# Hymba-style decoder step: sample attention by sample, its values gathered between later samples' keys

## The reference, cut to what matters

```python
D_MODEL, SEQ, DEC_BATCH, PAST_LEN, PAGE_SIZE = 1024, 512, 8, 4096, 128
N_HEADS, HEAD_DIM = 8, 64                  # cache: 320 pages of 128 x 8 x 64

def _fox_sample(q, k_new, v_new, logf_new, cache_k, cache_v, cache_logf, page_table):
    k_past = cache_k[page_table].reshape(bsz, past, N_HEADS, HEAD_DIM)
    v_past = cache_v[page_table].reshape(bsz, past, N_HEADS, HEAD_DIM)
    f_past = cache_logf[page_table].reshape(bsz, past, N_HEADS)
    ...
    cum = jnp.cumsum(jnp.concatenate([f_past, logf_new], axis=1), axis=1)
    s = jnp.einsum('bqhd,bkhd->bhqk', q, k_all) * (HEAD_DIM ** -0.5)
    s = s + cq - ck                        # forget sums behind each key
    p = jax.nn.softmax(s, axis=-1)
    return jnp.einsum('bhqk,bkhd->bqhd', p, v_all)

def _layer(x, c, ...):
    sh1, sc1, ga1, sh2, sc2, ga2 = _adaln(c, w_ada, b_ada, 6)
    h = _rms_norm(x, g_norm1) * (1.0 + sc1) + sh1
    q, k, v, logf, conv_in, gate_b = _mixer_inputs(h, w_in, b_forget)
    attn = attend(q, k, v, logf)           # prompt: causal, with the same forget sums
    conv_y, new_buf = _short_conv(conv_in, conv_buf, conv_w)
    x = x + ga1 * _merge_heads(attn, conv_y, gate_b, g_attn_out, g_conv_out, w_out)
    h = _rms_norm(x, g_norm2) * (1.0 + sc2) + sh2
    x = x + ga2 * _hier_moe(h, ...)        # top 2 of 32 experts, three 1 MB weights each
```

## Time and profile before

| | us |
|---|---|
| three runs | 1048.71, 1046.69, 1042.32 |
| their median | 1046.69 |
| span of the profiled execution | 1045.5 |
| TensorE busy | 847.3 (81%) |
| VectorE busy | 542.3 (52%) |
| POOL busy | 292.1 (28%) |
| ScalarE busy | 202.7 (19%) |
| moved by DMA | 318.40 MB, mean 305 GB/s |

### The profile page before, as it was taken

The page is one execution under the profiler, slowest core; times in us unless marked ns, Lnnn a source line. Parts: engine busy times, 40 slices in busy tenths (PEclk is TensorE's granted clock), DMA queues, the critical chain, the costliest instruction groups (busy, mean ns, idle before and its releaser), DMA issues.

```text
span 1045.5 us, 10030 instructions
## 1 busy us (share of the span) xinstructions
PE 847.3 (81%) x3810; PEld 371.9 (36%) x3810; DVE 542.3 (52%) x726; ACT 202.7 (19%) x385; POOL 292.1 (28%) x261
## 2 busy tenths in 40 slices
PE   7689999999457899998987989765888888778810
PEld 1144443444222334443232333223444444444300
DVE  1379999999999999642042020542111111111258
ACT  1321112100342322242000000121211222111111
POOL 4417632562101213102233232301222222221013
PEclk9689999999666575566999798876999999999955
DMA  9928778886779996616986999968999999999242
GB/s 332 399 90 290 285 281 340 275 304 207 261 276 335 371 382 249 222 41 256 361 341 267 359 333 358 373 254 294 389 410 413 412 411 412 412 412 413 107 176 82
DMA packets 79514, 318.40 MB, mean 305 GB/s; under 512 B 11090, under 2 KB 11110, under 8 KB 58473
## 3 DMA queue, kind: packets, MB, share of 16 engines
q1 hardware_dynamic: 52592, 163.56, 40.7%
q0 software_dynamic: 24576, 150.03, 38.3%
q10 hardware_dynamic: 2308, 4.31, 1.1%
HBM read 307.17 MB, written 14.85 MB: 308 GB/s over the span
## 4 chain that ended last, share of the span: by engine, by line
PE 65%; DMA 13%; DVE 11%; issue 6%; ACT 4%; SPq 1%; POOL 0%; ACTq 0%; POOLq 0%; DVEq 0%
PE bank L406 15%; PE bank L740 9%; PE bank L609 5%; PE bank L764 5%; DMA R_kv<-in_cache_v_dram,kv_index 5%; DMA R_w<-in_w_expert_up_dram 5%; PE bank L560 5%; PE bank L305 3%; PE bank L480 3%; PE bank L477 3%; PE bank L498 2%; DVE R_x L1232 2%; ACT R_h L861 2%; DMA R_w<-in_w_ada_dram 2%; DVE R_cm L1238 2%
## 5 line engine op out<-in xcount | busy, mean ns | idle before, releaser
L1732 POOL DMA_INDIRECT R_kv<-in_cache_k_dram,kv_index x64 | 98.6, 1540 | 244.6 <-DVE R_cm L1238 221.3
L1232 DVE TENSOR_TENSOR R_x<-R_kv,R_x 128x1024 f32<-128x1024 f32 x128 | 161.5, 1302 | 3.8 <-DMA R_x<-q_rows_scratch 3.8
L1238 DVE TENSOR_REDUCE R_cm<-R_x 128x16 f32<-128x1024 f32 x128 | 149.5, 1208 | 0.0
L406 PE MATMUL bank<-R_h,R_w 128*128 128x512 f32 x320 | 140.2, 599 | 1.2 <-ACT R_h L861 1.2
L1732 POOL DMA_INDIRECT R_kv<-in_cache_v_dram,kv_index x64 | 63.1, 986 | 166.3 <-PE bank L560 146.4
L560 PE MATMUL bank<-R_kv,R_cm 128*8 128x512 f32 x512 | 75.9, 676 | 19.8 <-DMA R_kv<-in_cache_v_dram,kv_index 19.6
L1808 POOL DMA_INDIRECT expert_rows_scratch<-R_h,R_part x32 | 32.0, 1001 | 211.6 <-DVE R_h L1593 204.2
L406 PEld LDWEIGHTS bank<-R_h,R_w 128*128 128x128 f32 x320 | 61.0, 192 | 79.9 <-issue 78.3
L1590 DVE COPY R_h<-bank 128x128 f32<-128x128 f32 x32 | 9.3, 292 | 147.0 <-PE bank L756 147.0
L305 PE MATMUL bank<-R_w,R_q 128*32 128x512 f32 x256 | 51.8, 938 | 13.8 <-DMA R_w<-in_w_ada_dram 8.2
L1593 DVE TENSOR_SCALAR R_h<-bank,R_part 128x512 f32<-128x512 f32 x32 | 24.0, 751 | 70.6 <-PE bank L764 70.6
(11 more groups left out here) (329 smaller groups left out, 1345.0 us busy)
## 6 DMA issues: line engine op xcount, KB each, us to landing
R_w<-in_w_ada_dram SPq DMA_DIRECT2D x24, 1024.0 KB, 8.1
R_w<-in_w_in_dram SPq DMA_DIRECT2D x12, 1024.0 KB, 7.7
R_w<-in_w_ada_final_dram SPq DMA_DIRECT2D x8, 1024.0 KB, 10.2
R_kv<-in_w_expert_gate_dram SPq DMA_DIRECT2D x8, 1024.0 KB
R_kv<-in_w_expert_up_dram SPq DMA_DIRECT2D x8, 1024.0 KB
R_kv<-in_w_expert_down_dram SPq DMA_DIRECT2D x8, 1024.0 KB
R_q<-in_w_expert_gate_dram SPq DMA_DIRECT2D x8, 1024.0 KB
R_q<-in_w_expert_up_dram SPq DMA_DIRECT2D x8, 1024.0 KB
```

The source lines that it names most:

```text
L406: last = nc.tensor.matmul(bank[m][:, :], l, r, start=(k == 0), stop=(k == KD - 1))
L1232: V.tensor_tensor(prod[:, r, :], kv_ring[:, n % RING, r, :], spread(q, [P, CH // 2, HW]), ALU.mult)\
L1238: V.reduce_sum(scores[:, b, lo:lo + CH // 2, :], prod[:, r, :].rearrange("p r (h d) -> p r h d", h=H), AX.X).then_inc(S["k_used"], 1)
L1732: pool.indirect_dma_start(kv_flat[:, g % RING, :], None, k_rows if g < NKV else v_rows, bass.IndirectOffsetOnAxis(kv_index[:, n:n + 1], 0))\
```

## The change

Keys and values share the four places in one order that is written out ahead (`kv_seq`): 16 key chunks, then values between keys, one value to 1.08 keys up to value 22, then one to one, and the last 18 values. Each sample has its own softmax, two key chunks after its last key: maximum (`sample_top`), reduction over partitions on POOL, subtraction (`sample_shift`), exponentials (`sample_exp`), sum (`sample_sum`). Value chunks stand on TensorE at 23 places inside sections 2 to 5, at each of the 32 attention steps, and nine behind them. Key products are written over the keys; the first sample's q is spread by a matmul. The log-forget sums and the new row are made on VectorE. Five modulation chunks move from attention into sections 0 to 2, with places of their own (`a_unit`). Sections use two PSUM banks in pairs, scores two and turned probabilities one. Output tiles stand whole behind each other, the samples ahead of tile 3, and routing is done once for all five tiles.

```diff
-        NEW_AT, DIAG_AT = 16, 32
-        ADA_AT = {w: n for n, w in enumerate((0, 1, 3, 4, 6, 8, 10, 12, 14, 16, 19, 22))}
+        def value_at(m):
+            if m < 5:
+                return 15.5 + m
+            if m < 23:
+                return 21.5 + (m - 5) * 19.5 / 18
+            return 41.0 + (m - 23)
+
+        order = sorted([(float(n), 0, n) for n in range(NKV)] + [(value_at(m) + 0.3, 1, m) for m in range(NKV)])
+        kv_seq = [(("k", "v")[kind], i) for _, kind, i in order]
+        ring_slot = [g % RING for g in range(2 * NKV)]
+        ring_prev = [g - RING if g >= RING else None for g in range(2 * NKV)]
...
+        EARLY = 5
+        ADA_AT = {w: EARLY + n for n, w in enumerate((7, 10, 12, 15, 17, 20, 22))}
+        VALUES_AFTER = {2: (3, 4, 5, 6, 7), 3: (1, 2, 3, 5, 6, 7), 4: (1, 2, 3, 5, 6, 7), 5: (1, 2, 3, 5, 6, 7)}
+        LATE = (0, 1, 2, NT, 3)
...
             def prompt_section(s):
+                for pair in range(2):
+                    for half in range(2):
+                        w = use_unit(8 + 2 * s + half)
+                        for m in (2 * pair, 2 * pair + 1):
+                            e = 4 * s + m - 2
+                            if half == 0 and 0 <= e < 16:
+                                pe.wait_ge(S["acc_act"], e + 1)
+                            if half == 0 and e >= 16:
+                                pe.wait_ge(S["acc_dve"], e - 15)
...
+                            block = 4 * pair + 2 * half + m % 2
+                            if block in VALUES_AFTER.get(s, ()):
+                                values(1)
+                    if pair == 0 and s < 3:
+                        early_ada(2 * s)
+                if s < 2:
+                    early_ada(2 * s + 1)
...
             for w in range(NT * H):
                 turn(w)
                 if w + 2 < NT * H:
                     score(w + 2)
-                if w >= NT * H - V_EARLY:
-                    value_chunk(w - (NT * H - V_EARLY))
+                values(1)
                 weigh(w)
...
+            values(1)
+            turn_output(NT - 1)
+            values(1)
+            spread_chunk(2)
...
+            gather_values(6)
+            for half in range(2):
+                for k0 in range(0, KD, 2):
+                    out_part(0, half, k0)
+                    if next_v[0] < NKV:
+                        values(1)
+            sample_sums()
+            gather_values(7)
+            for t in (1, 2):
+                for half in range(2):
+                    for k0 in range(0, KD, 2):
+                        out_part(t, half, k0)
+                turn_rows(t - 1)
+                route(t - 1)
+                if t == 1:
+                    sample_head_squares()
+            out_samples()
+            for half in range(2):
+                for k0 in range(0, KD, 2):
+                    out_part(3, half, k0)
+            for i in (2, 3, 4):
+                turn_rows(i)
+                route(i)
...
             def k_chunk(n):
...
-                for i in range(2):
-                    if n:
-                        dve.wait_ge(S["k_used"], 2 * n - 1 + i)
-                    r = slice(i * CH // 2, (i + 1) * CH // 2)
-                    V.tensor_tensor(prod[:, r, :], kv_ring[:, n % RING, r, :], spread(q, [P, CH // 2, HW]), ALU.mult)\
-                        .then_inc(S["k_products"], 1)
+                keys = kv_ring[ring_slot[g]]
+                V.tensor_tensor(keys[:, :, :], keys[:, :, :], spread(q, [P, CH, HW]), ALU.mult).then_inc(S["k_products"], 1)
+                dve.wait_ge(S["k_products"], n + 1)
+                V.reduce_sum(scores[:, b, s * CH:(s + 1) * CH, :], keys.rearrange("p r (h d) -> p r h d", h=H), AX.X)\
+                    .then_inc(S["k_used"], 1)
...
+            def decay_step(i):
+                d = 1 << i
+                out = decay[:, :, 0:PPP - d, :]
+                last = V.tensor_tensor(out, out, decay[:, :, d:PPP, :], ALU.add)
...
             def cache_chunk(g):
-                n = g % NKV
-                if g >= RING:
-                    pool.wait_ge(*((S["k_used"], 2 * (g - RING + 1)) if g - RING < NKV else (S["v_used"], g - RING - NKV + 1)))
+                kind, n = kv_seq[g]
+                if ring_prev[g] is not None:
+                    before, i = kv_seq[ring_prev[g]]
+                    pool.wait_ge(S["k_used" if before == "k" else "v_used"], i + 1)
...
+            for g in range(RING, 2 * NKV):
+                kind, n = kv_seq[g]
+                if kind == "k" and n % NCH == 0:
+                    query(n // NCH)
                 cache_chunk(g)
+                for b in turn_after.get(g, ()):
+                    pool.wait_ge(S["top_part"], b + 1)
+                    G.partition_all_reduce(top_all[:, b, :], top[:, b, :], P, RED.max).then_inc(S["top_ready"], 1)
...
-            free = ((S["v_used"], NKV), (S["wo_part_done"], 2), (S["lg_done"], 5), (S["h2_ready"], 5))
+            free = ((S["v_used"], NKV), (S["wo_done"], 2 * NT), (S["lg_done"], 5), (S["h2_ready"], 5))
```

830 lines of the change are left out of this document (472 added, 358 removed).

## The result

The changed kernel takes 1091.6 us (median of four runs, 1086.3 to 1096.5), the kernel before, run beside it, 1047.2 (four runs, 1042.3 to 1048.7): a ratio of 1.043, 95% interval 1.038 to 1.048. It is slower by 44 us, where 12 us less were forecast, and lies above the forecast's range. The profiled execution spans 1084.1 us; the one before spanned 1045.5. In all that follows medians count every run, while ratios and their intervals leave out the slow runs, those over 1.5% above the fastest run of the same kernel.

The account below looks back on a forecast made before the run. No single engine was full throughout; VectorE was the clock before the loop, weights paced the experts. +47 until the loop, +29 in it and -87 behind gave -11: 1034.5 us profiled, 1035 as median, range 1005 to 1064.

Parts of the forecast that it names:

- The rest, 0: Experts and last norm, after the tables are copied out: no change from 330.3 us.
- Behind the loop, 141: From the loop's last weighing to the tables: 227.7 us falls to 141, with only 9 value chunks left there.
- The term of 6 us for each of two turns: Behind the loop: turn and route of a tile between output tiles, waiting for a norm, 6 us each, 12 together.
- Until the loop, 47 more: From the start to the first row maximum: 274.65 us grows to 322.
- At 175: Before the loop: VectorE at its 18th key chunk at 167 us, 175 with waits for forget path and ring.
- All of them at 6.4: From 175 us to the loop: 23 pairs of key and value at 6.4 us each.
- (landing + 4.53)/2: Ring before the loop: least cost of a key and value pair; a landing of 8.3 us gives 6.4.
- The loop, 29 more: The 32 attention steps: 212.9 us grows to 242, as 63 + 118 + 61.
- In place, the same cost: Key products before the loop: writing over the key chunk costs the same 4.53 us, a gain of at most 0.1.
- Log-forget sums, +5 net: Before the loop: additions moved to VectorE add 9.2 + 2.2 us; POOL's removed additions give back about 6.
- B: Rival, sections and loop: the ring costs more than it gives, pairs above 6.7 us, 1074 us; chance 0.18.
- A: Rival, loop: mostly full TensorE clock, loop 219 us, total 1012 us; chance 0.22.

Follow-up runs that it names:

- e11_act: On e4_three, ScalarE's copy of a tile's turned rows put ahead of the next tile's norm, first two tiles behind the loop; 1043.7 us, ratio to kernel before 0.997.
- e1_order: Changed kernel with early modulation chunks 1 and 3 moved behind the forget gate's projection and the turns of the log-forget rows; 1074.7 us.
- e4_three: Changed kernel with all three edits (e1_order, e2_ring5, e3_conv) in one kernel; 1048.0 us, ratio to kernel before 1.001.
- e6_early0: Changed kernel with no modulation chunks beside the sections, all twelve back in the loop; 1074.3 us, ratio to kernel before 1.033.
- e2_ring5: Changed kernel with a fifth place in the key and value ring, given up after the last key; 1074.5 us, ratio to kernel before 1.033.
- e3_conv: Changed kernel with the value chunk of loop steps 0 to 4 moved behind the sums of the convolution's squares; 1074.7 us, ratio to kernel before 1.030.
- b1_inplace: Kernel before with only the key product written over the key chunk, one whole product and reduction instead of two halves; 1051.4 us, ratio 1.008.
- e7_poolsum: Changed kernel with the five doubling additions over the log-forget sums back on POOL; 1091.3 us, ratio to kernel before 1.044.
- e5_late: On e4_three, eight of the sixteen value chunks of loop steps 8 to 23 moved behind the loop; 1046.9 us, ratio to kernel before 1.004.

## Why the prediction was wrong, step by step

**The rest, 0: nearly right** (+3.6 us in the one execution; 331.4 with three edits, so part of it is spread between executions; where the remainder lies wasn't looked for). No term of the sum stood for it.

**Behind the loop, 141: right in sum** (142.3, and 141.9 to 148.3 over ten traces with the clock; the bounds were 135 and 152). The term of 6 us for each of two turns was seen as such: 3.6 of it is the wait, of which e11_act removed 2.4.

**Until the loop, 47 more: the step that failed** (81.6 more). Three terms of it, with 20.4 + 8.5 + 5.3 us:
- "At 175": the working, 62 + 18 x 4.53 + 23, has 18 chunks done by then, so it answers to the start of the 19th, and with 23 more the count of 41 before the loop is right. The 19th starts at 195.4, +20.4. With the order mended it starts at 176.4 (e1_order), with all three edits at 173.2 (e4_three): the count of the work was right, and what failed was that the early modulation chunks were taken to delay nobody. The prediction said of the early modulation units that "each is due a whole section before its successor is needed". That was an argument on SP's queue alone. It left out that a unit's buffer is free only with the chunk before, that on the chain the landing is 12 to 14 us (the page's median is 11.6 for these units, 9.2 for one in R_w), and that the forget gate's projection and the log-forget rows stand behind these chunks on TensorE, with VectorE waiting for both (e1_order, e6_early0).
- All of them at 6.4: one is 14.9, where VectorE does the convolution's products between two key chunks, +8.5. In the kernel before the same gap is there, 14.8 us (238.01 to 252.85), so the old trace had this term. With four places just two keys are ahead, so little is stored up in this time.
- The pair itself: 6.64 for the other 22, +5.3 (356.3 - 195.4 - 14.9 = 146.0, over 22). To 240 us, where bytes bind, it is the forecast's 6.4; most of the excess is the 10 pairs behind, at 6.8, where the transfers had room and a fifth place helped. The landing on the chain is 9.3 us rather than 8.3, and POOL's issue, 0.94 to 2.9 us, was priced in the text but is not in (landing + 4.53)/2. With both in, that formula gives 7.4 and more, so it isn't confirmed either: not every pair waits for a landing on the chain. In the last pairs VectorE waits 4.1 us for a section's matmuls, which stand behind a value chunk that has not landed. With five places a pair is 6.2 (e2_ring5) and 6.4 (e4_three), counted the same way.

**The loop, 29 more: failed in its first eight steps** (38.8 more). Steps 24 to 31 were right, and so were steps 8 to 23 (114.4 for 118, bound by bytes as forecast). Steps 0 to 7 got 3 us more for the softmax pieces and took 15.8. The term left out is the value chunk in the chain of the convolution's norm: 6.9 of it (e3_conv). The other 6 weren't told apart; with that edit what remains over the kernel before lies mostly in steps 0 and 1 (3.1 and 2.1 us).

**In place, the same cost: right for VectorE's rows, wrong for POOL's** (b1_inplace). **Log-forget sums, +5 net:** about right at the 18th key chunk (6.0 earlier without them), though the time shows nothing of it (e7_poolsum).

**The rivals.** B came nearest: slower, and with pairs of 7.0 us on average against its limit of 6.7, though its 1074 is 18 us short. That it is so near is in part luck: its mechanism is the 14 us that a fifth place gives back, of some 41. The delay at 175 and the chain in the loop are no matter of the ring, and no rival had them. Its picture of the value that waits for TensorE fits worse: from 60 to 356 us POOL waited 160.9 us for VectorE's use of a key chunk and 27.0 for TensorE's of a value. A did not come: the clock was 0.52 up to w = 8 and 0.66 up to w = 24. The Trainium skill (TensorE: Matmul & The Clock Gate, What's actually happening) has idle time throttle the array; in steps 1 to 4, with an idle 6 us in each, the value chunks do run at half clock (1.90 us), and behind the waits of e5_late too, so here the traces agree.

So what the trade gives was priced rightly, and of its cost the bytes of steps 8 to 23 and VectorE's own work. What made it a loss was where five weight chunks and five value chunks stand in TensorE's order, and a ring with a place too few for two streams.

## What to carry to other kernels

When work is moved into an engine's gaps, write down for each moved instruction what stands behind it on that engine and who waits for that, its weights' landing included: here two such places and a ring that was too short held some 41 us, nearly all that was lost, and each was cured by a swap of a few lines or by one more buffer. A ring that was sized for one stream has half its depth for each of two, so every long piece of other work by its consumer stands bare. Before a ring is blamed, ask whether the transfers have room: from 195 to 240 us here they had none, and a fifth place gained nothing there. And a stretch that is bound by bytes gives back what is taken out of it, but the stretch that received it grew by more than the work, by 1.8 to 2.7 us for a chunk of 1.04, of which the granted clock has a share that one trace can't separate.

## What the runs showed of the hardware

- POOL's issue of a list of descriptors stretches with VectorE's products of two SBUF inputs: 0.94 us beside none, mostly 1.64 to 1.72 or 2.8 beside two halves of 1.2 us each, up to 3.04 beside a whole product of 2.28. An issue that starts while the product runs ends about 0.8 us after the product does, whenever it started:

```profile
208.07 2.29 DVE L1356 TENSOR_TENSOR R_kv<-R_kv,R_x 128x2048 f32<-128x2048 f32 x1 [0.70 <-DMA R_kv<-in_cache_k_dram,kv_index]
```
```profile
207.64 0.94 POOL L1948 DMA_INDIRECT R_kv<-in_cache_v_dram,kv_index  x1 [5.19 <-DVE R_cm L1358]
208.88 2.29 POOL L1948 DMA_INDIRECT R_kv<-in_cache_k_dram,kv_index  x1 [0.30 <-issue]
```

  Up to 356 us the changed kernel has 15 stretched issues beside key products, and 14 of them end 0.81 to 0.83 us behind the product's end (one 0.96); in b1_inplace, up to 230 us, all 28 end 0.80 to 0.87 behind it. An issue that starts up to 0.8 us ahead of the product, as at 207.64, isn't stretched. So the issue waits for the end of a product that is already running. The Trainium skill (SBUF — State Buffer, Who interferes with whom) expects such a product not to stall an issue, and notes that this is inferred; these rows speak against it. It does expect such a product and a POOL operation that reads SBUF to hold each other up, and here the traces agree (5.13 us for a product of 2.28).
- Runs of one kernel follow, in the main, the clock that was granted on average: with three edits 1036.6 us at 0.857 and 1056.1 at 0.835. The kernel before, in 25 runs, goes from 1039.9 at 0.856 to 1051.1 at 0.836, though its slowest run, 1051.8, had 0.849. The stretch from the last weighing to the tables, the same work with the same long waits, takes 141.9 us at 0.86 in one trace and 148.3 at 0.81 in another. What moves the granted clock from run to run is open.
- Key, value and weight transfers together moved 416 to 422 GB/s over 45 us (195 to 240 us, three traces), a little more than the 413 of the expert weights.
